# A hybrid decoder trunk on one Trainium2 core: the mLSTM tile's columns copied one tile ahead, and three steps of a projection stream moved within a GLA tile

## What is computed

```python
def _gla_core(seqs, s0):            # HGRN2 and GLA: q, k, log_a per head and key; v; state s
    def step(s, inp):
        qc, kc, vc, ac = inp
        b = jnp.cumsum(ac, axis=1)
        decay = jnp.exp(jnp.where(mask, b[:, :, None] - b[:, None], -jnp.inf))
        att = jnp.einsum('bthk,bshk,btshk->bhts', qc, kc, decay)
        o = jnp.einsum('bhts,bshv->bthv', att, vc) + jnp.einsum('bthk,bhkv->bthv', qc * jnp.exp(b), s)
        s = s * jnp.exp(bl)[..., None] + jnp.einsum('bshk,bshv->bhkv', kc * jnp.exp(bl[:, None] - b), vc)

def _mlstm_core(seqs, state):       # mLSTM with a running maximum m_t as stabiliser
        wts = jnp.exp(dmat - m_t[:, :, None])
        qk = jnp.einsum('bthk,bshk->btsh', qc, kc) * wts
        num = jnp.einsum('btsh,bshv->bthv', qk, vc) + sc[..., None] * jnp.einsum('bthk,bhkv->bthv', qc, cm)
        den = jnp.sum(qk, axis=2) + sc * jnp.einsum('bthk,bhk->bth', qc, nm)
        hc = num / jnp.maximum(jnp.abs(den), jnp.exp(-m_t))[..., None]
```

## Time and profile before

| | |
|---|---|
| three runs, median (lowest to highest) | 2546.67 us (2542.06 to 2553.62) |
| the profiled execution, its own time | 2545.37 us |
| its span, first to last instruction | 2543.8 us |
| TensorE clock granted, mean over the span | 0.933 of full speed |
| PE busy | 2269.4 us, 89% of the span |
| DVE busy | 1176.0 us, 46% |
| ACT busy | 675.8 us, 27% |

### The profile page before, as it was taken

How to read it: one execution, slowest core, us unless ns; L and a number is a source line. 1 busy time by engine, 2 the same in 40 slices (tenths; PEclk the granted TensorE clock), 3 DMA queues, 4 the chain that set the end, 5 groups by cost and what they waited for, 6 DMA issues and landing times.

```text
span 2543.8 us, 34492 instructions
## 1 busy us (share of the span) xinstructions
PE 2269.4 (89%) x13669; PEld 2156.7 (85%) x13669; DVE 1176.0 (46%) x1973; ACT 675.8 (27%) x1071; POOL 183.5 (7%) x339
## 2 busy tenths in 40 slices
PE   4998988799999789999998868899999997999996
PEld 3977778789898688888888867899999997999995
DVE  5423331566666444444444357652222224555565
ACT  5222112323232043333333044101100102333342
POOL 1000011131222100000000021100000001000000
PEclk8988899899899889999999879999999998999998
DMA  4111125212121221111111055412111224111112
GB/s 162 43 51 51 40 44 120 91 50 75 58 68 58 73 84 44 42 42 45 42 42 41 16 194 180 138 44 108 48 42 41 62 89 181 42 41 41 41 41 86
DMA packets 82632, 178.25 MB, mean 70 GB/s; under 512 B 10464, under 2 KB 50096, under 8 KB 82320
## 3 DMA queue, kind: packets, MB, share of 16 engines
q1 hardware_dynamic: 67056, 123.35, 15.5%
q0 software_dynamic: 15488, 54.13, 6.5%
q10 hardware_dynamic: 32, 0.01, 0.0%
HBM read 129.43 MB, written 48.02 MB: 70 GB/s over the span
## 4 chain that ended last, share of the span: by engine, by line
PE 75%; DVE 11%; ACT 5%; DMA 4%; issue 3%; POOL 1%; POOLq 0%; DVEq 0%; ACTq 0%; SPq 0%
PE PS L450 20%; PE PS L451 19%; PE PS L452 19%; PE PS L941 2%; DMA AR<-zrows 2%; PE PS L1059 2%; PE PS L1055 2%; PE PS L1049 2%; DMA orows<-AR 1%; DVE AR L1824 1%; DVE AR L2186 1%; DVE AR L2059 1%; DVE AR L1822 1%; ACT AR L1352 1%; ACT AR L1382 1%
## 5 line engine op out<-in xcount | busy, mean ns | idle before, releaser
L450 PE MATMUL PS<-HT_parts,W_parts 128*128 128x358 f32 x1440 | 531.7, 369 | 14.9 <-ACT AR L501 10.9
L451 PE MATMUL PS<-OT_parts,W_parts 128*128 128x358 f32 x1440 | 494.4, 343 | 0.0
L452 PE MATMUL PS<-HT_parts,W_parts 128*128 128x358 f32 x1440 | 492.3, 342 | 0.0
L450 PEld LDWEIGHTS PS<-HT_parts,W_parts 128*128 128x128 f32 x1440 | 294.4, 204 | 25.4 <-ACT AR L501 11.4
L451 PEld LDWEIGHTS PS<-OT_parts,W_parts 128*128 128x128 f32 x1440 | 293.3, 204 | 2.2
L452 PEld LDWEIGHTS PS<-HT_parts,W_parts 128*128 128x128 f32 x1440 | 291.4, 202 | 0.0
L450 PE MATMUL PS<-ACT_parts,CF_parts 128*128 128x358 f32 x768 | 255.6, 333 | 26.5 <-DVE ACT_parts L532 16.0
L450 PE MATMUL PS<-HN_parts,CF_parts 128*128 128x358 f32 x768 | 251.3, 327 | 4.7 <-DVE OT_parts L532 4.7
L452 PE MATMUL PS<-HN_parts,RING_parts 128*128 128x358 f32 x768 | 250.9, 327 | 0.0
L452 PE MATMUL PS<-ACT_parts,RING_parts 128*128 128x358 f32 x768 | 250.8, 327 | 0.0
L451 PE MATMUL PS<-OT_parts,CF_parts 128*128 128x358 f32 x768 | 250.7, 326 | 0.0
(11 more groups left out here) (385 smaller groups left out, 3696.3 us busy)
## 6 DMA issues: line engine op xcount, KB each, us to landing
RING<-in_w_all SPq DMA_DIRECT2D x132, 512.0 KB, 3.7
zrows<-AR SPq DMA_DIRECT2D x162, 179.0 KB, 1.9
AR<-zrows POOLq DMA_DIRECT2D x32, 537.0 KB, 3.8
AR<-zrows SPq DMA_DIRECT2D x8, 640.0 KB, 4.5
AR<-in_xT SPq DMA_DIRECT2D x8, 537.0 KB, 7.1
HT<-in_xT POOLq DMA_DIRECT2D x8, 537.0 KB, 6.8
residual<-HT POOLq DMA_DIRECT2D x8, 537.0 KB, 6.5
acts<-AR POOLq DMA_DIRECT2D x8, 537.0 KB, 3.3
```

The source lines that it names most:

```text
L450: e.matmul(out, whi, xhi, start=first, stop=False)
L451: e.matmul(out, whi, xlo, start=False, stop=False)
L452: return e.matmul(out, wlo, xhi, start=False, stop=last)
```

## The change

It has two parts that do not touch each other.

1. **mLSTM.** MC becomes MC2 with two halves; tile n uses half n mod 2. ACT copies tile 0's columns ahead of the loop, and the columns of tile n+1 within tile n, behind the square of `o_sq` and ahead of the first of the tile's evacuations. ACT's loop runs three times over two tiles instead of four, and the last two full tiles are written out. To make room, MQH and MX move to rows of the same region that are dead by then.
2. **GLA.** On PE, in all tiles but the last, seven steps of the stream instead of four stand between the diagonal products and level 1. A tile still has 24 steps, so three remain after `o_normed`'s transposes instead of six. The other engines' programs are the same.

```diff
-        MC = a.take(s=6, t=P)
+        MC2 = a.take(u=2, s=6, t=P)
...
-        MX = a.take(h=4, t=P)
-        MQH = a.take(h=4, t=P)
+
+        MQH = Arena(KEEPTO, KEEPTO + W).take(h=4, t=P)
+        MX = Arena(KEEPTO + 2 * W, KEEPTO + 3 * W).take(h=4, t=P)
...
-            def ml_tile(n, w, work, last_tile=False):
+            def ml_tile(n, u, w, work, last_tile=False):
+                MC = MC2[:, u]
...
-                    ml_tile(i * 2 + u, P, stream(e, i + J_ML, u))
-            ml_tile(TILES, LASTW, stream_pair(e, J_MLT), True)
+                    ml_tile(i * 2 + u, u, P, stream(e, i + J_ML, u))
+            ml_tile(TILES, 0, LASTW, stream_pair(e, J_MLT), True)
...
-                steps(work, 4)
+                steps(work, 4 if last_tile else 7)
...
-            def ml_tile(n, w, j, us):
+            def ml_columns(m, u, w):
+                src = M4[:, :, TILES * P:NT] if w < P else M4[:, :, bass.ds(m * P, P)]
+                e.wait_ge(S("ml_pre"), m)
+                e.activation(MC2[:, u, :, 0:w], src, ACT.Copy).then_inc(S("ml_copied"), 1)
+            e.wait_ge(S("ml_pre"), 1)
+            e.activation(MC2[:, 0], M4[:, :, 0:P], ACT.Copy).then_inc(S("ml_copied"), 1)
+
+            def ml_tile(n, w, j, us, w_next):
...
-                src = M4[:, :, TILES * P:NT] if last_tile else M4[:, :, bass.ds(n * P, P)]
-                e.wait_ge(S("ml_pre"), n + 1)
-                e.activation(MC[:, :, 0:w], src, ACT.Copy).then_inc(S("ml_copied"), 1)
                 e.wait_ge(S("k_turned"), n + 1)
...
                 e.activation(MSQ[0:w], num, ACT.Square, scale=0.125).then_inc(S("o_sq"), 1)
+                if w_next:
+                    ml_columns(n + 1, 1 - us[0], w_next)
                 evacs(1)
...
-            with e.Fori(0, TILES // 2) as i:
+            with e.Fori(0, TILES // 2 - 1) as i:
                 st.enter(i, 2)
                 for u in range(2):
-                    ml_tile(i * 2 + u, P, i + J_ML, (u,))
-            st.leave(TILES // 2)
-            ml_tile(TILES, LASTW, J_MLT, (0, 1))
+                    ml_tile(i * 2 + u, P, i + J_ML, (u,), P)
+            st.leave(TILES // 2 - 1)
+            ml_tile(TILES - 2, P, J_ML + TILES // 2 - 1, (0,), P)
+            ml_tile(TILES - 1, P, J_ML + TILES // 2 - 1, (1,), LASTW)
+            ml_tile(TILES, LASTW, J_MLT, (0, 1), 0)
```

More of the change, by code:

```diff
@@ L1696, in ml_tile @@
                     e.wait_ge(S("ml_copied"), TILES + 1)
-                    e.tensor_tensor(MQX, bc(MC[:, 2, 0:w].unsqueeze(1), [P, SEGS, w]),
+                    e.tensor_tensor(MQX, bc(MC2[:, 0, 2, 0:w].unsqueeze(1), [P, SEGS, w]),
                                     const("ind_t").rearrange("p (s t) -> p s t", s=SEGS), ALU.mult).then_inc(S("tail_q"), 1)
```

## The result

| | before | after |
|---|---|---|
| time, median (lowest to highest) | 2548.94 us (2542.06 to 2553.62), 4 runs | 2465.04 us (2460.64 to 2466.25), 4 runs |
| ratio after/before, 95% interval | | 0.967 (0.9643 to 0.9697) |
| profiled execution, its span | 2545.37, 2543.8 us | 2460.64, 2459.1 us |
| granted TensorE clock, mean | 0.933 | 0.954 |
| PE busy | 2269.4 us | 2222.9 us |

Lines have moved: PE's L849, L941 and L994 are L851, L943 and L996 now; L1352, L1811, L1822, L1824, L1825, L1834, L1848 and L1856 of ACT and DVE stand ten lines further down; L501, L717 and L719 one. DVE and ACT do the same work as before. PE is busy for 46.5 us less with the same number of products; with that goes the higher mean clock, 0.954 after 0.933.

What follows compares the result with a forecast made beforehand. PE was taken to bound the kernel (75% of the last-ending chain), through its waits and lower clock; 17.5 + 21.9 + 8.5 + 2.9 + 15 = 65.8 us off the profiled 2545.4 gave 2480 us, range 2462 to 2508.

Steps and rivals of the forecast that it cites:

- the other side of rival 2: GLA: the whole level-2 wait goes, 7 x 1.8 us and the held-back 6 us of clock more, 2461 us; chance 0.04.
- rival 2: GLA: the level-2 wait hardly shrinks because ACT's earlier finish meets another bound, 2504 us; chance 0.06.
- mLSTM's clock: mLSTM tiles: PE's clock stays up once the head wait goes, six tiles of seven, 21.9 of 25.6 us.
- GLA's chain: GLA tiles 1 to 7: ACT freed sooner by the shorter tail, level-2 wait 3.0 to 1.8, 1.2 us a tile, 8.5 us.
- GLA's clock: GLA tiles: with level-2 waits of 1.8 us PE's clock mostly stays up, two of seven still falling, 15 of 21 us.
- mLSTM's waits: mLSTM tile heads: PE's wait for ACT's column copy goes in all tiles but the first, 17.5 of 19.8 us.
- The reserve of one tile in seven: mLSTM: only six tiles of seven were counted as getting their clock back, 21.9 us of 25.6.
- The last tile: GLA's last tile: reached with nine steps instead of twelve, so its levels start 2.9 us earlier.
- 1 (4-row products): mLSTM: PE's 4-row products bring the clock down by themselves, 21.9 us more, 2502 us; chance 0.10.
- 3 (short waits still cost the clock): GLA: the shorter level-2 waits still cost the clock each time, the 15 us stay, 2495 us; chance 0.08.
- 4 (too short a tail): GLA: with three tail steps PE stops at the next tile's first step for the fifth group's bank, slower; chance 0.02.

Runs made afterwards that it cites:

- the last kernel: The changed kernel with tile 0's mLSTM column copy ahead of the last evacuation and weight split, and DVE's L1835 and L1844 behind level 0's masked copies: 2458.18 us.

## Why the prediction came out as it did

Predicted 2480 us, measured 2465.04; the time is inside the range of 2462 to 2508, but 3 us below the forecast's own range of 2468 to 2493. It lies nearer to the other side of rival 2 (the whole GLA wait goes, 2461), which had been given 0.04. Sign and mechanism were right; three terms were too small (mLSTM's clock, GLA's chain and GLA's clock), and some 4.5 us of the profiled gain are luck.

- **mLSTM's waits, 17.5 us:** right. 19.8 became 2.3, and nothing that the prediction named next (`ml_gbd`, ACT's weight split, the rstd) shows up as a wait.
- **mLSTM's clock, 21.9 us of 25.6:** the stretch of the earlier trace rows is 40.7 us shorter, of which 15.3 are its waits (17.5 less tile 1's, which lies ahead of it), so 25.4 are clock. The reserve of one tile in seven was 3.5 us too much. But the doubled products show that the reserve was no idle caution: with twice the 4-row products about 9.7 us are lost again.
- **GLA's chain, 8.5 us:** the step that failed. The 1.2 us for ACT's earlier start are right (1.26: L1362 starts 7.94 us after L996 where its counterpart started 9.20 us after L994; over seven tiles that is 8.8). But the rest of the chain was taken with the durations of the trace before, and these held a contention: DVE's last products lay beside GpSimd's. Moved 1.26 us earlier they start ahead of GpSimd's and take about 0.8 us less. Each tile gains 2.03 us of wait, 14.2 in all, 5.7 more than counted. The rows for it stood in the trace of before, the same product at 0.35 and at 0.56 us (556.73 and 557.27, above).
- **The last tile, 2.9 us:** right, 3.0.
- **GLA's clock, 15 us of 21:** the stretch of the earlier trace rows is 35.0 us shorter; 3.0 are the last tile's earlier start and 12.2 six waits of 2.03, so 19.8 are clock, and PEclk is 1.00 in it. That is 4.8 us more than counted. The argument for it was thin: a wait of 1.83 us in the last mLSTM tile had cost nothing, so 1.8 here would not. The runs contradict such a transfer: 1.25 us, with 1.9 us of 4-row products behind them, cost the clock in four mLSTM tiles of seven (behind the 1.83 us there were only 0.8 us of such products, 341.26 to 342.03 in the trace of before), and with 2.15 us GLA's tiles stood at 0.92 and 0.96. The clock that came back came back at waits of 0.97, not 1.8; what 1.8 would have cost was not measured, so that part of the forecast was met without its argument being borne out.
- **Luck:** 84.7 - 65.8 = 18.9 us came on top of the forecast in the profiled execution. Of these 3.8 are mLSTM's tiles and 10.6 GLA's (5.7 and 4.8 by the terms above). The rest, about 4.5, is the landing of one transfer and the earlier start of the stage, neither of which the prediction had or, by the rows, the change made.

The rivals: 1 (4-row products) is a real mechanism that 1.9 us of them did not set off. 2 (ACT meets another bound) did not occur: ACT met the one bound that the sum had already put there, L1821, and the wait shrank by more than was counted, to about half of the 1.8 us that the sum left. 3 (short waits still cost the clock) does not hold at 0.97 us and does at 2.15. The rule that was cited for it, the Trainium skill's "TensorE: Matmul & The Clock Gate", section "A second HAM failure mode: psum-queue depth-cycling", says that often-repeated short idling swings the clock; the rows agree for waits of 1.25 us with short-row products behind them and for 2.15, not for 0.97. 4 (too short a tail) did not occur in any full tile from 1 on; the wait of 7.0 us for an evacuation in tile 0 takes the place of one of 10.6.

## What to carry to other kernels

When a chain ends a wait, ask for each of its instructions what ran beside it, and look for the same instruction elsewhere in the trace at another duration: moved by a microsecond, it may have another length. Free an engine only as far as the next bound: the first of the three moved steps gave nearly all, and two products moved on the engine that became the bound took the rest of the wait. Price a wait together with the short-row products next to it, because the clock answers to both, and keep a case in which all of its cost comes back.

## What the runs showed of the hardware

- **DVE beside GpSimd.** A product of two SBUF operands, 128x192, takes 0.35 us alone and 0.56 to 0.79 beside GpSimd's products; 128x384 takes 0.55 alone, 0.75 and 0.97 beside them. The Trainium skill, "SBUF — State Buffer", section "Who interferes with whom", says that a VectorE instruction with two SBUF inputs contends with a GpSimd instruction that reads SBUF. The rows agree with the contention: L1844 was lengthened by 0.42 us beside a GpSimd product that began ahead of it and that the trace gives 0.93. Begun 0.17 us ahead of a GpSimd product, in after, it kept its 0.55.
- **The clock falls without waiting.** It fell, with PE busy throughout, behind 3.7 us of 4-row products in six tiles of seven. Behind 2.6 us of 32-row products it fell in three of seven tiles of the last kernel, in two of seven with 5, 6 and 8 steps, and in none with 7: the same work falls in one tile and not in the next.
- **One transfer, many durations.** The same rows sent out from GpSimd's queue landed after 15.3 to 21.9 us. As PE waits for them, that moves the end by several microseconds from one execution to the next.
